# A layer's mixer, first half: the work put in the order rows, recurrence chunks, recurrent branch, gated convolution, and the gated convolution computed on GpSimd

## The reference, cut to what matters

```
cols = x @ w_in
A: sparse attention; a small indexer scores all keys, the top 128 (129) of each row are kept
B: z = p + (prev - p) * mu;  r, k, v, wl, al, gl = split(z)
   decay = f(tanh(wl) @ w2), a = sigmoid(al @ a2), g = sigmoid(gl) @ g2     # low-rank products
   kk = k*kkw / max(norm(k*kkw), 1e-12);  kf = k * (1 + (a-1)*ka)
   s = s*decay + (s @ -kk) (kk*a) + v kf;  y = (groupnorm(s @ r) + (sum r*kf*rk) * v) * g
C: bg, cg, xin = split(p);  y = bg * conv3(cg * xin)                        # gated convolution
D: xb, gb = split(p);  xc = conv4(xb) + b
   gate_x, gate_a = sigmoid(xc @ gx + ..), sigmoid(xc @ ga + ..)
   log_a = -8 * gate_a * softplus(-lam)
   h = exp(log_a) * h + sqrt(-expm1(2 log_a)) * gate_x * xc;  y = h * gelu(gb)
x = LN(alpha*x + concat(A, B, C, D) @ w_out);  x = LN(alpha*x + moe(x))
```

## Time and profile before

| | us |
|---|---|
| median of 3 timed runs (1805.0 to 1808.62) | 1807.95 |
| the profiled execution | 1809.34 |
| its span, first to last instruction | 1807.8 |
| PE busy | 1297.8 |
| DVE busy | 741.0 |
| ACT busy | 302.6 |
| POOL busy | 146.5 |

### The profile page before, as it was taken

How to read it: one execution, slowest core, us unless ns; L and a number is a source line. 1 busy time by engine, 2 the same in 40 slices (tenths; PEclk the granted TensorE clock), 3 DMA queues, 4 the chain that set the end, 5 groups by cost and what they waited for, 6 DMA issues and landing times.

```text
span 1807.8 us, 23389 instructions
## 1 busy us (share of the span) xinstructions
PE 1297.8 (72%) x8400; PEld 819.7 (45%) x8400; DVE 741.0 (41%) x1494; ACT 302.6 (17%) x692; POOL 146.5 (8%) x167
## 2 busy tenths in 40 slices
PE   5999732963797299995299995359467964989922
PEld 2678622942446244442147783159243462444412
DVE  0247998445124211111803599974531341111126
ACT  1121122202201011111112201402131000111101
POOL 0300000002101200001300000000030112000022
PEclk9999956986796599998599997679678956999975
DMA  5392001004540368885511120010056003878841
GB/s 214 117 404 71 24 0 37 4 1 129 180 172 1 122 233 324 317 333 194 187 52 62 59 71 0 1 39 4 25 166 268 23 1 139 332 301 315 324 156 49
DMA packets 67254, 246.35 MB, mean 136 GB/s; under 512 B 8050, under 2 KB 28690, under 8 KB 58002
## 3 DMA queue, kind: packets, MB, share of 16 engines
q1 hardware_dynamic: 47536, 174.90, 26.2%
q0 software_dynamic: 13424, 47.77, 7.4%
q10 hardware_dynamic: 6194, 22.36, 3.1%
HBM read 194.36 MB, written 52.87 MB: 137 GB/s over the span
## 4 chain that ended last, share of the span: by engine, by line
PE 34%; issue 32%; DVE 15%; DMA 7%; POOL 5%; DVEq 2%; POOLq 2%; ACT 1%; SPq 0%; PEldq 0%; ACTq 0%
PE ps L1056 10%; PE ps L578 7%; PE ps L558 6%; PE ps L1073 5%; DMA arena<-in_w_dn 5%; DVE arena L1962 4%; DVE arena L1958 3%; POOL arena L481 2%; PE ps L997 2%; POOL arena L532 1%; DVE arena L1577 1%; POOLq L509 1%; DMA arena<-in_wa 1%; POOL arena L510 1%; POOL rows_in L522 1%
## 5 line engine op out<-in xcount | busy, mean ns | idle before, releaser
L1136 ACT ACTIVATE arena<-ps 128x512 f32<-128x512 f32 (+11 forms) x404 | 173.7, 471 | 824.3 <-PE ps L578 205.4
L578 PE MATMUL ps<-arena 128*128 128x272 f32 x1088 | 257.8, 396 | 0.0
L1056 PE MATMUL ps<-arena 128*128 128x512 f32 x512 | 229.6, 600 | 13.2 <-DMA arena<-in_w_dn 10.8
L578 PEld LDWEIGHTS ps<-arena 128*128 128x128 f32 x1088 | 206.9, 191 | 48.5 <-issue 4.0
L680 PE MATMUL ps<-arena 64*64 64x64 f32 (+3 forms) x4016 | 154.1, 237 | 63.4 <-DVEq L1743 53.0
L680 PEld LDWEIGHTS ps<-arena 64*64 64x64 f32 x4016 | 139.7, 137 | 76.2 <-DVEq L1743 53.2
L1056 PEld LDWEIGHTS ps<-arena 128*128 128x128 f32 x512 | 97.1, 192 | 141.3 <-issue 136.9
L1073 PE MATMUL ps<-arena 128*128 128x512 f32 x256 | 117.5, 601 | 19.5 <-DVE arena L2219 19.5
L558 PE MATMUL ps<-arena 128*128 128x512 f32 (+1 forms) x256 | 104.4, 570 | 19.6 <-DMA arena<-in_wa 19.1
L1010 PE MATMUL ps<-arena 128*128 128x512 f32 x256 | 114.1, 607 | 2.0 <-ACT arena L1136 2.0
L2215 DVE TENSOR_TENSOR arena<-arena,ps 128x256 f32<-128x256 f32 x32 | 13.5, 423 | 238.6 <-ACT arena L1412 238.6
(11 more groups left out here) (335 smaller groups left out, 1296.4 us busy)
## 6 DMA issues: line engine op xcount, KB each, us to landing
arena<-in_w_gu SPq DMA_DIRECT2D x32, 2048.0 KB, 8.0
arena<-in_w_dn SPq DMA_DIRECT2D x32, 1024.0 KB, 11.0
arena<-in_wf SPq DMA_DIRECT2D x34, 512.0 KB, 3.4
arena<-rows_in SPq DMA_DIRECT2D x32, 512.0 KB, 3.4
rows_out<-arena ACTq DMA_DIRECT2D x32, 512.0 KB, 6.0
rows_in<-arena POOLq DMA_DIRECT2D x12, 1024.0 KB, 24.7
arena<-in_cache_k SPq DMA_DIRECT2D x64, 128.0 KB, 2.6
arena<-in_cache_v POOLq DMA_DIRECT2D x64, 128.0 KB, 2.5
```

The costliest lines, as they stand in the source:

```text
L578: mm = pe.matmul(ps[:, 2 + 2 * h + n % 2, 0:HALF], m.wf[n % 3][:, c, :], m.xT[:, c, h * HALF:h * HALF + HALF], start=c == 0, stop=c == KC - 1)
L1056: mm = pe.matmul(ps[:, 3, :], m.xgT[:, c, :], m.w_gu[k][:, c, :], start=c == 0, stop=c == KC - 1)
L1136: return act.activation(out, in_, ACT.Copy)
```

## The change

The chunks' order becomes B's seven (as 6, 2, 3, 0, 1, 4, 5: the low-rank inputs first, then the keys), D's four, C's six. On PE the products of `column_jobs` are spread among the chunks: the low-rank ones behind chunk 2, key norms behind 8, bonus sums behind 9, D's gate products behind 11. The two products for B's output gate move behind the first group norm product, and DVE reads them from PSUM. ACT's order follows; it also writes `Z` scaled by 1 - mu, so that the token mix is one DVE operation, and writes D's gate chunks straight to their place. DVE's order becomes mix and keys, scores, 2 rounds, first half of D's convolution, key norms, chunk inputs, second half, 4 rounds, D's branch in three portions with a round between each two, 3 rounds, 6 rounds, closing pass. C's convolution leaves DVE and is computed on POOL, with a tensor_scalar and an addition for each tap. ACT waits for `fc_used` ahead of copying chunks 15 and 16, and DVE ahead of its first mask. For the decay's input the factor 1 - a² is computed from the squared decay in place of a formula with a reciprocal. Regions of `arena` are laid out anew for this. The recurrence itself stays as it is.

```
+MIXED = (6, 2, 3, 0, 1, 4, 5)
+GATES = {8: 0, 10: 1}
...
-        sp.wait_ge(s["state_room"], nth(l, "state_room", 1))
+        sp.wait_ge(s["fm_mm"], nth(l, "fm_mm", NCH))
...
+    def taps(out, tmp, src, w):
+        width = SEQ if len(src.shape) == 2 else DS
+        def at(k):
+            return src[:, 1 + k:1 + k + width] if len(src.shape) == 2 else src[:, :, 1 + k:1 + k + width]
+        pool.tensor_scalar(out, at(0), w[0], None, mul)
+        for k in range(1, 3):
+            pool.tensor_scalar(tmp, at(k), w[k], None, mul)
+            pool.drain()
+            pool.tensor_tensor(out, out, tmp, add)
+            pool.drain()
+    def conv_c(l, j):
+        convc = m.param("convc").rearrange("p (j b t) -> p j b t", j=2, b=DB)
+        tail = m.small("convc").rearrange("p (j c) -> p j c", j=2)
+        cw = m.param("cw")
+        n = 11 + 3 * j
+        cg, xin, bg = n % 4, (n + 1) % 4, (n + 2) % 4
+        pool.wait_ge(s["fm_copied"], nth(l, "fm_copied", n + 3))
+        pool.tensor_tensor(m.turn, m.const("ones"), m.const("ones"), ALU.add)
+        pool.drain()
+        pool.tensor_copy(m.fm_s[cg][:, :, 1:3], convc[:, j, :, :])
+        pool.drain()
+        pool.tensor_tensor(m.fm_p[cg][:, 3:3 + SEQ], m.fm_p[cg][:, 3:3 + SEQ], m.fm_p[xin][:, 3:3 + SEQ], mul)
+        pool.tensor_tensor(m.fm_s[cg][:, :, 3:7], m.fm_s[cg][:, :, 3:7], m.fm_s[xin][:, :, 3:7], mul)
+        pool.drain()
+        w = [cw[:, 3 * j + k:3 * j + k + 1] for k in range(3)]
+        taps(m.conv[:, 0:SEQ], m.tap[:, 0:SEQ], m.fm_p[cg], w)
+        taps(seqs(m.conv[:, SEQ:T]), seqs(m.tap[:, SEQ:T]), m.fm_s[cg], w)
+        pool.tensor_copy(tail[:, j, 0:2], m.fm_p[cg][:, 1 + SEQ:3 + SEQ])
+        pool.tensor_copy(tail[:, j, 2:18].rearrange("p (b t) -> p b t", t=2), m.fm_s[cg][:, :, 5:7])
+        pool.drain()
+        pool.tensor_tensor(m.yT[:, 4 + j, 0:SEQ], m.conv[:, 0:SEQ], m.fm_p[bg][:, 3:3 + SEQ], mul)
+        pool.tensor_tensor(seqs(m.yT[:, 4 + j, SEQ:T]), seqs(m.conv[:, SEQ:T]), m.fm_s[bg][:, :, 3:7], mul).then_inc(s["fc_used"], 1)
...
+        conv_c(l, 0)
+        conv_c(l, 1)
+        pool.drain()
...
+    def product(l, job, lhsT, rhs):
+        if job >= 2:
+            pe.wait_ge(s["job_out"], nth(l, "job_out", job - 1))
+        width, b = rhs.shape[1], 6 - 6 * (job % 2)
+        pe.matmul(ps[:, b, :], lhsT, rhs[:, 0:SEQ], start=True, stop=True)
+        pe.matmul(ps[:, b + 1, 0:width - SEQ], lhsT, rhs[:, SEQ:width], start=True, stop=True).then_inc(s["job_mm"], 1)
+    def loras(l):
         pe.wait_ge(s["lora_act"], nth(l, "lora_act", 1))
-        for w in ("gxw", "gaw"):
+        pe.wait_ge(s["tr_copied"], nth(l, "tr_copied", 6))
+        pe.wait_ge(s["tr_sample"], nth(l, "tr_sample", 2))
+        for a, rows in enumerate((slice(0, 32), slice(32, 64))):
+            for p in range(2):
+                product(l, 2 * a + p, m.param("lora")[rows, 128 * p:128 * p + 128], m.Z[rows, 6, :])
+    def key_norms(l):
+        pe.wait_ge(s["kk_in"], nth(l, "kk_in", 1))
+        pe.wait_ge(s["s_score"], nth(l, "s_score", 1))
+        for p in range(2):
+            product(l, 4 + p, m.const("ones_head"), m.bv[:, p, :])
+    def bonuses(l):
+        pe.wait_ge(s["bonus_in"], nth(l, "bonus_in", 1))
+        for p in range(2):
+            product(l, 6 + p, m.const("ones_head"), m.bonus[:, p, :])
+    def lru_gates(l):
+        for a, w in enumerate(("gxw", "gaw")):
             for p in range(2):
                 pe.wait_ge(s["conv_done"], nth(l, "conv_done", p + 1))
+                product(l, 8 + 2 * a + p, m.param(w)[:, 128 * p:128 * p + 128], m.xc[:, p, :])
+    def projections(l):
+        row_projection(l)
+        pe.wait_ge(s["const_in"], 64)
+        pe.wait_ge(s["params_in"], nth(l, "params_in", 16))
+        columns(l, 0, 1)
+        head_transposes(l, 0)
+        columns(l, 2)
+        head_transposes(l, 3)
+        loras(l)
+        columns(l, 3)
+        sample_indexer(l)
+        columns(l, 4)
+        indexer(l, 3)
+        columns(l, 5)
+        indexer(l, 2)
+        columns(l, 6)
+        indexer(l, 1)
+        columns(l, 7)
+        sample_scores(l)
+        columns(l, 8)
+        key_norms(l)
+        columns(l, 9)
+        bonuses(l)
+        columns(l, 10, 11)
+        lru_gates(l)
+        columns(l, 12, 13, 14, 15, 16)
...
+        pe.wait_ge(s["fm_copied"], nth(l, "fm_copied", NCH))
+        pe.wait_ge(s["job_out"], nth(l, "job_out", 12))
...
+            if step == 0:
+                for p in range(2):
+                    w = m.param("lora")[64:128, 128 * p:128 * p + 128]
+                    pe.matmul(ps[:, 4 + 2 * p, :], w, m.Z[64:128, 6, 0:SEQ], start=True, stop=True)
+                    mm = pe.matmul(ps[:, 5 + 2 * p, 0:NS], w, m.Z[64:128, 6, SEQ:T], start=True, stop=True)
+                mm.then_inc(s["yn_mm"], 1)
...
+        columns(l, 0, 1)
+        head_columns(l, 0)
+        columns(l, 2)
+        head_columns(l, 3)
+        act.wait_ge(s["fm_used"], nth(l, "fm_used", 1))
+        act.activation(m.Z[0:32, 6, :], m.Z[0:32, 6, :], ACT.Tanh)
+        act.activation(m.Z[64:128, 6, :], m.Z[64:128, 6, :], ACT.Sigmoid).then_inc(s["lora_act"], 1)
+        for p in range(2):
+            job(l, p, m.ea[:, p, :], ACT.Sigmoid, TP, m.param("w0")[:, p:p + 1])
+        for p in range(2):
+            job(l, 2 + p, m.aa[:, p, :], ACT.Sigmoid, TP, m.param("a0")[:, p:p + 1])
+        columns(l, 3)
+        sample_indexer(l)
+        act.wait_ge(s["cum_ready"], nth(l, "cum_ready", 1))
+        act.activation(m.ea, m.ea, ACT.Exp, scale=-DECAY)
+        act.activation(m.ec, m.en, ACT.Exp, scale=-DECAY)
+        act.activation(m.en, m.en, ACT.Exp, scale=DECAY).then_inc(s["exps_ready"], 1)
+        columns(l, 4)
+        relus(l, 3)
+        columns(l, 5)
+        relus(l, 2)
+        columns(l, 6)
+        relus(l, 1)
+        columns(l, 7)
+        sample_scores(l)
+        columns(l, 8)
+        for p in range(2):
+            job(l, 4 + p, m.bv[:, p, :], ACT.Sqrt, TP)
+        columns(l, 9)
+        for p in range(2):
+            job(l, 6 + p, m.bonus[:, p, :], ACT.Copy, T)
+        columns(l, 10, 11)
+        for p in range(2):
+            job(l, 8 + p, m.gx[:, p, :], ACT.Sigmoid, T, m.param("gxb")[:, p:p + 1])
+        for p in range(2):
+            job(l, 10 + p, m.za[:, p, :], ACT.Sigmoid, T, m.param("gab")[:, p:p + 1])
+        columns(l, 12, 13)
+        act.wait_ge(s["dz_ready"], nth(l, "dz_ready", 1))
+        act.activation(m.za_tanh, m.za, ACT.Tanh)
+        act.activation(m.a_lru, m.za, ACT.Exp, scale=-1.0).then_inc(s["d_tanh"], 1)
+        act.wait_ge(s["gelu_in"], nth(l, "gelu_in", 1))
+        act.activation(m.gelu, m.gelu, ACT.Tanh, scale=GELU_C).then_inc(s["gelu_tanh"], 1)
+        columns(l, 14)
+        act.wait_ge(s["om_ready"], nth(l, "om_ready", 1))
+        act.activation(m.za, m.za, ACT.Sqrt).then_inc(s["om_sqrt"], 1)
+        columns(l, 15, 16)
...
+            if n in GATES:
+                gb = m.gb[:, GATES[n], :]
+                copy(gb[:, 0:HALF], first)
+                copy(gb[:, HALF:T], second).then_inc(s["fm_copied"], 1)
+                continue
+            if n >= 15:
+                act.wait_ge(s["fc_used"], nth(l, "fc_used", 1))
...
+                z = MIXED[n]
+                copy(shift[:, z, 0:1], second[:, SEQ - HALF - 1:SEQ - HALF])
+                copy(shift[:, z, 1:9], sample[:, :, DS - 1])
+                act.activation(m.Z[:, z, 0:HALF], first, ACT.Copy, scale=m.rest[:, z:z + 1])
+                act.activation(m.Z[:, z, HALF:T], second, ACT.Copy, scale=m.rest[:, z:z + 1])
...
+    def mix(l, *chunks):
+        mu = m.param("mu")
+        shift = m.param("shift").rearrange("p (n b) -> p n b", b=DB)
+        for n in chunks:
+            z = MIXED[n]
+            fp, fs, zs = m.fm_p[n % 4], m.fm_s[n % 4], seqs(m.Z[:, z, SEQ:T])
+            dve.tensor_copy(fs[:, :, 2], shift[:, z, :])
+            dve.drain()
+            dve.wait_ge(s["fm_copied"], nth(l, "fm_copied", n + 1))
+            stt(m.Z[:, z, 0:SEQ], fp[:, 2:2 + SEQ], mu[:, z:z + 1], m.Z[:, z, 0:SEQ], mul, add)
+            stt(zs, fs[:, :, 2:6], mu[:, z:z + 1], zs, mul, add).then_inc(s["fm_used"], 1)
+    def key_squares(l):
+        k = m.Z[:, 2:4, :]
+        dve.drain()
+        for p in range(2):
+            ts(m.nkk[:, p, :], k[:, p, :], m.param("kkw")[:, p:p + 1], None, mul)
+        dve.drain()
+        tt(m.bv, m.nkk, m.nkk, mul).then_inc(s["kk_in"], 1)
+    def decays(l):
+        dve.wait_ge(s["job_out"], nth(l, "job_out", 2))
+        for p in range(2):
+            dve.tensor_tensor_scan(m.en[:, p, :], m.const("reset"), m.ea[:, p, :], 0.0, mul, add)
+        dve.drain()
+        tt(m.ea, m.en, m.ea, sub).then_inc(s["cum_ready"], 1)
+    def key_rates(l):
+        dve.wait_ge(s["job_out"], nth(l, "job_out", 4))
+        for p in range(2):
+            ts(m.kf[:, p, :], m.aa[:, p, :], m.param("ka")[:, p:p + 1], m.omka[:, p:p + 1], mul, add)
+        dve.drain()
```

(112 more changed lines are left out.)

244 lines of the change are left out of this document (66 added, 178 removed).

## The result

The changed kernel takes 1780.31 us (median of 4, 1776.89 to 1785.19) where the kernel before takes 1808.28 beside it. The ratio is 0.984, 95% interval 0.981 to 0.988: 28 us faster. A second set of the same kernel gave 0.986 (0.982 to 0.990). The forecast was 1795, so the time lies in the range, the sign is right, and the gain is twice the 13 to 14 us forecast.

What follows compares the result with a forecast made beforehand. DVE's list was taken to bound the stretch ahead of each recurrence. Per layer 27.8 − 15 + 4.8 − 2.7 − 8 = 6.9 us, 13.8 in both, giving 1795 us; range 1774 to 1818, the forecast's own 1786 to 1804.

Steps and rivals of the forecast that it cites:

- The bound: Stretch ahead of each layer's recurrence: bound by DVE's list, 161.4 us in one piece from the indexer's last scores.
- Items 1 and 2: DVE's list: 17.0 us a layer taken off, 10.8 moved ahead of its start, together 27.8 shorter.
- item 5: Recurrence start: PE's early products remove DVE's 3.81 us wait and some queueing, 4.8 us a layer gained (2.5 to 6).
- Item 3: Low-rank products between chunks 2 and 3: PE idle and lower clock start DVE's list 15 us later a layer (10 to 22).
- Item 4: PE's moved products and a standstill: column chunks end at 241 us instead of 213, hidden by 55 us of slack.
- Item 6: Output gate at the group norm: two more products and PSUM reads on the path cost 2.7 us, 4.9 if PE is cold.
- Item 7: GpSimd's convolutions beside DVE's recurrent branch: mutual exclusion costs DVE 8 us a layer, bounds 0 and 20.
- A: Rival on GpSimd beside DVE: its work falls into selection rounds, costing next to nothing; 1779 us, chance 0.25.
- B: Rival on GpSimd beside DVE: selection operations wait too, 20 us a layer, slower at 1819 us; chance 0.18.
- C: Rival on PE's chunks up to the scores: lower clock throughout, list 22 us later, 1809 us, no change; chance 0.15.

Runs made afterwards that it cites:

- e8: The changed kernel without the last three selection rounds (`select_rounds(6)` becomes `select_rounds(3)`): 1766.94 us, ratio 0.979 to the kernel before.
- e2: The changed kernel with GpSimd's gated convolution left out, only zeros written to its outputs, waits and order kept: 1774.4 us, ratio 0.981 to the kernel before.
- e9: The changed kernel with DVE's group norm wait split, gate products awaited only ahead of its last multiplication: 1769.32 us, ratio 0.979 to the kernel before.
- e3: The changed kernel with the second convolution's large taps on GpSimd done four times, beside selection rounds: 1783.26 us, ratio 0.988 to the kernel before.
- e4: The changed kernel with the first convolution's large taps on GpSimd done three times, beside the recurrent branch: 1783.4 us, ratio 0.988 to the kernel before.

## Why the prediction was wrong, point by point

*The bound* was right: DVE's list, shown by e8, and by PE's 46 us wait.

*Items 1 and 2*, the list shorter by 27.8, were right. From start to first mask it went from 165.24 to 135.17; without GpSimd's work (e2) 133.42, that is 31.8 less, of which 3.8 is the head start of item 5 and 28.0 the list.

*Item 3*, the later start: 15 forecast, 13.6 measured. PE's rows:

```profile
106.31 2.07 PE L683 MATMUL ps<-arena 32*128 32x512 f32 x2 [5.29 <-ACT arena L1239]
...
111.86 2.02 PE L683 MATMUL ps<-arena 32*128 32x512 f32 x2
...
114.13 9.60 PE L623 MATMUL ps<-arena 128*128 128x272 f32 x32
...
126.63 7.64 PE L623 MATMUL ps<-arena 128*128 128x272 f32 x32
...
374.67 1.10 PE L968 MATMUL ps<-arena 128*128 128x512 f32 x2 [0.89 <-DVE arena L1980]
...
382.38 2.08 PE L968 MATMUL ps<-arena 128*128 128x512 f32 x2 [3.08 <-DVE arena L1990]
```

Idle 5.29 (5.3 forecast), products 7.8 from 106.31 to 114.13 (8), next chunk 9.60 for 7.64 (1.4 forecast, 2.0 measured). The chunk behind the sample indexer, 9.06 in the earlier trace rows, was at 7.64 this time, which gave 1.4 back.

*Item 4*, the column chunks late and hidden: the chunks end at 240.7 (241 forecast; eight products at 1.2 are 9.6 and not 9.4), and nothing on the path waited for them.

*Items 5 and 6*, the head start and the gate: the wait of 3.81 is gone; from mask to memset it is 2.35 and 3.0 longer, for 1.7 by the two items together. Item 5 gave 4.5 and 3.9 instead of 4.8: the 3.81, and a recurrence 0.7 and 0.1 shorter. The 1.0 forecast for that did not come in full, since PE now starts behind its wait of 46 us at a lower clock. Ten us behind the first mask, before and after:

```profile
312.50:322.50 10.00, 10.00 (x274) 10.00 (x274) 7.68 (x14) 1.20 (x2) 0.00 (x0) 1.00 0.01 3
296.00:306.00 10.00, 7.34 (x164) 7.34 (x166) 7.49 (x14) 1.20 (x2) 0.00 (x0) 0.68 0.02 4
```

Item 6 cost 3.0 and 3.1 instead of 2.7. The row at 382.38 has the reason: the variance products run wholly at the lower level, 2.08 where the first of them took 1.45 before. e9 shows both the wait's part and this one.

*Item 7* is the step that failed, and by its size: "each of about eight large operations waits for roughly 1 us: 8 us" was 1.75. The mechanism is right: the operations exclude each other, as the earlier trace rows showed, and e3's and e4's held rows show it again. Two things in the picture were wrong. The number of times that DVE waits: two, not eight. GpSimd was triggered 2.5 us into the first portion, but the dummy addition, two drains and a small copy stand ahead of its first large operation, which began 3.5 us later, inside a round; the second convolution ran beside rounds alone, since DVE had already ended the branch at 243.6. That the first large product fell into a round was luck: the same four steps took 0.67 us at the second convolution, and 2.08 of the 3.5 are an idle ahead of the copy that stands in the first layer of every trace with this code, e2's too (1.5 in the second layer); no run shows its cause. And the side that waits: I charged DVE for every meeting, as in the earlier trace rows where a single GpSimd operation had a head start. The engines met more than twice, but when DVE's operations follow one another within 0.1 us, GpSimd's wait as well, through two of them in the row of 3.53. That 6.25 us a layer, 12.5 in both, with the 1.4 of item 3 and less the 0.7 to 1.3 of items 5 and 6, makes the 6.9 forecast into 13.3 to 13.9 a layer. The traces have 14.1 at the first layer's memset and 27.2 at the second's; the medians differ by 28.0.

The Trainium skill's rule ("SBUF — State Buffer", section "Who interferes with whom") is that a DVE operation with at most one SBUF input, outside the two-port modes, does not contend with GpSimd. e3 agrees with it: MAX8 and MATCH_REPLACE8 unchanged over 24 us; in which mode they run, no row shows. The Trainium skill's "GPSIMD Engine Reference", section "4.1 Engine selection", puts two-input work on GpSimd at about twice DVE's time, and the trace agrees: 1.27 on 512 against 0.69. The Trainium skill's "1-input is roughly line-rate" in the same section is not what this kernel's row shows: the tensor_scalar on 512 took 1.57, more than the two-input one, and above my bound of 1.2. It cost nothing, since GpSimd's own length was not on the path.

*The rivals.* A, free of charge, had the right time (1779), and nearly the right reason: the operations fell into the rounds. B is refuted by e3. C did not happen: the chunks from 126.63 on took 7.64.
